# State-space mixer: a group's inputs and outputs turned between tokens and steps by 16 small ScalarE instructions instead of 16 TensorE products

## The reference

```python
def s5_mixer(h, w_in, ...):
    u = h @ w_in                                    # [256 tokens, 1024] = 64 groups of 16 channels
    for each chunk of steps:
        bu = einsum('bcgn,gpn->bcgp', u_c, bb)      # complex, 64 states a group
        s  = scan(s_t = lambda * s_{t-1} + bu_t)
        y  = real(einsum('bcgp,gnp->bcgn', s, c))
    y = y + d_skip * u
    g = gelu(y)
    g = g * sigmoid(g @ w_glu)
    return g @ w_out
```

## Time and profile before

| | |
|---|---|
| median of 3 runs | 1701.78 us (1699.98 to 1702.68) |
| the profiled execution | 1702.0 us, its span 1700.4 us |
| TensorE busy | 1682.7 us, 99% |
| VectorE busy | 1322.7 us, 78% |
| ScalarE busy | 875.4 us, 51% |
| GpSimd busy | 377.0 us, 22% |
| granted TensorE clock | full in all 40 slices |

### The profile page before, as it was taken

How to read it: one execution, slowest core, us unless ns; L and a number is a source line. 1 busy time by engine, 2 the same in 40 slices (tenths; PEclk the granted TensorE clock), 3 DMA queues, 4 the chain that set the end, 5 groups by cost and what they waited for, 6 DMA issues and landing times.

```text
span 1700.4 us, 29659 instructions
## 1 busy us (share of the span) xinstructions
PE 1682.7 (99%) x11608; PEld 1520.6 (89%) x11608; DVE 1322.7 (78%) x1813; ACT 875.4 (51%) x1280; POOL 377.0 (22%) x425
## 2 busy tenths in 40 slices
PE   9999999999999999999999999999999999999999
PEld 8899999898889998888888998888888899988887
DVE  7897889885868889787896868886688765678773
ACT  5875444353665444455544256554555435556552
POOL 0232012535514313600032130002100137330000
PEclk9999999999999999999999999999999999999999
DMA  8246567675116787555636445565455644335560
GB/s 336 94 146 216 202 212 271 231 270 197 60 50 217 250 270 268 183 201 179 227 142 260 130 154 184 182 242 176 145 201 199 221 151 169 122 127 199 200 244 25
DMA packets 50709, 320.98 MB, mean 189 GB/s; under 512 B 7696, under 2 KB 8912, under 8 KB 20144
## 3 DMA queue, kind: packets, MB, share of 16 engines
q1 hardware_dynamic: 36432, 280.61, 46.3%
q0 software_dynamic: 12736, 36.87, 6.8%
q10 hardware_dynamic: 1440, 2.10, 0.3%
HBM read 307.39 MB, written 10.09 MB: 187 GB/s over the span
## 4 chain that ended last, share of the span: by engine, by line
PE 89%; DVE 7%; DMA 2%; ACT 1%; issue 1%; POOL 0%; SPq 0%; ACTq 0%; DVEq 0%
PE bank L2363 35%; PE bank L2364 17%; PE bank L2357 9%; PE bank L2358 8%; PE bank L2359 8%; DVE w_lo L1495 2%; PE bank L2583 1%; PE bank L2690 1%; PE bank L3062 1%; PE bank L3014 1%; PE bank L2767 1%; PE bank L2596 1%; PE bank L2703 1%; PE bank L2880 1%; ACT w_hi L1041 1%
## 5 line engine op out<-in xcount | busy, mean ns | idle before, releaser
L1495 DVE TENSOR_TENSOR w_lo<-raw,w_hi 128x1024 fp32r<-128x1024 f32 (+2 forms) x486 | 640.8, 1321 | 178.5 <-ACT w_hi L1041 176.5
L1041 ACT ACTIVATE w_hi<-raw 128x1024 fp32r<-128x1024 f32 (+2 forms) x486 | 538.2, 1113 | 401.4 <-PE bank L2364 229.2
L2363 PE MATMUL bank<-hg,w_hi 128*128 128x512 f32 x1408 | 491.9, 395 | 0.0
L2364 PE MATMUL bank<-hg,w_lo 128*128 128x256 f32 x1408 | 391.6, 278 | 0.0
L2363 PE MATMUL bank<-hid,w_hi 128*128 128x512 f32 x1056 | 372.1, 396 | 2.5 <-DVE h L1540 1.5
L2357 PE MATMUL bank<-hg,w_hi 128*128 128x256 f32 x1240 | 354.2, 286 | 1.1 <-ACT u_s L1420 0.8
L2358 PE MATMUL bank<-hg,w_hi 128*128 128x256 f32 x1240 | 350.8, 283 | 0.0
L2359 PE MATMUL bank<-hg,w_lo 128*128 128x256 f32 x1240 | 350.7, 283 | 0.0
L2363 PEld LDWEIGHTS bank<-hg,w_hi 128*128 128x128 f32 x1408 | 264.2, 188 | 62.5
L2364 PE MATMUL bank<-hid,w_lo 128*128 128x256 f32 x1056 | 296.7, 281 | 0.0
L2364 PEld LDWEIGHTS bank<-hg,w_lo 128*128 128x128 f32 x1408 | 264.8, 188 | 0.1
(11 more groups left out here) (431 smaller groups left out, 2240.0 us busy)
## 6 DMA issues: line engine op xcount, KB each, us to landing
raw<-in_w SPq DMA_DIRECT2D x189, 1024.0 KB, 4.8
raw<-in_w SPq DMA_DIRECT2D x48, 1408.0 KB, 6.1
raw<-in_w SPq DMA_DIRECT2D x8, 768.0 KB, 4.8
b_rows<-in_s_b_rows POOLq DMA_DIRECT2D x8, 512.0 KB, 8.1
l_rows<-s_powers POOLq DMA_DIRECT2D x64, 64.0 KB, 9.2
s_ca<-cp_s POOLq DMA_DIRECT2D x8, 512.0 KB, 4.4
s_ba<-ba_s POOLq DMA_DIRECT2D x8, 512.0 KB, 7.4
ba_slot<-s_ba POOLq DMA_DIRECT2D x8, 512.0 KB, 5.5
```

The source lines that it names most:

```text
L1041: act.activation(w_hi[s][:, 0:n], raw[r][:, c * n:(c + 1) * n], ACT.Copy).then_inc(hi_made, 1)
L1495: dve.tensor_tensor(w_lo[s][:, 0:n], raw[r][:, c * n:(c + 1) * n], w_hi[s][:, 0:n].bitcast(F32), ALU.subtract).then_inc(lo_made, 1)
L2363: pe.matmul(psum[:, :].rearrange("p (a t) -> p a t", a=2), w_hi_ap, x_pair, start=first, stop=False)
L2364: return pe.matmul(psum[:, 0:T], w_lo_ap, x_pair[:, 0, :], start=False, stop=last)
```

## The change

All four `turn_inputs` and the first three `turn_outputs` leave TensorE. In their place ScalarE gets `turn_inputs(r)`: 16 activations, each of 32 partitions and 2 x 64 elements, which copy one step of one quarter of both tiles from `u_s` (every fourth element) to the 32 partitions of that step in `u4_s`. And it gets `gelu_to_steps(r)` for r = 0 to 2: 16 activations, each of which takes 32 partitions and 128 elements of the bank of `chunk_outputs(r)` through the gelu and writes them to every fourth element of `u_s`; then the high part is made as before. Group 3 keeps the old way out. TensorE's and ScalarE's orders are written anew, and on VectorE `keep_u(2)` goes ahead of `states(0)`.

```diff
--- before.py
+++ after.py
@@ -614,7 +614,6 @@
         z_read = sem("z_read")
         z_scanned = sem("z_scanned")
         h_made = sem("h_made")
-        u4_turned = sem("u4_turned")
         g_made = sem("g_made")
         g_turned = sem("g_turned")
         g_kept = sem("g_kept")
@@ -1400,10 +1399,32 @@
                     for j in range(a, b):
                         split_hi(half0 + j + SPLIT)
 
-                def keep_chunk_rows(r):
-                    act.wait_ge(u4_turned, r + 1)
-                    act.activation(u4_s[:, 2 * r:2 * r + 2, :, :], y_bank(r)[:, :].rearrange("p (k q c) -> p k q c", k=2, q=4), ACT.Copy)\
-                       .then_inc(u4_made, 1)
+                def quarter(i):
+
+                    return slice(32 * i, 32 * i + 32)
+
+                def turn_inputs(r):
+
+                    act.wait_ge(u_made, r + 1)
+                    for q in range(4):
+                        u = by_chunk(u_s[quarter(q), 2 * r:2 * r + 2, :])
+                        for step in range(LC):
+                            last = act.activation(u4_s[quarter(LC - 1 - step), 2 * r:2 * r + 2, q, :], u[:, :, :, step], ACT.Copy)
+                    last.then_inc(u4_made, 1)
+
+                def gelu_to_steps(r):
+
+                    if r == 0:
+                        act.wait_ge(half_used, half0 + 8)
+                    act.wait_ge(ca_used, 2 * r + 2)
+                    for q in range(4):
+                        g = by_chunk(u_s[quarter(q), 2 * r:2 * r + 2, :])
+                        for step in range(LC):
+                            y = y_bank(r)[quarter(step), :].rearrange("p (k q c) -> p k q c", k=2, q=4)
+                            last = act.activation(g[:, :, :, step], y[:, :, q, :], ACT.Gelu_apprx_tanh)
+                    last.then_inc(g_kept, 1)
+                    act.wait_ge(g_kept, r + 1)
+                    act.activation(hg_hi[:, 2 * r:2 * r + 2, :], u_s[:, 2 * r:2 * r + 2, :], ACT.Copy).then_inc(ghi_made, 1)
 
                 def gelu(r):
 
@@ -1413,9 +1434,7 @@
                                    ACT.Gelu_apprx_tanh).then_inc(g_made, 1)
 
                 def hi_of_g(r):
-                    if r == 0:
-                        act.wait_ge(half_used, half0 + 8)
-                    act.wait_ge(g_turned, r + 1)
+                    act.wait_ge(g_turned, 1)
                     g = u_s[:, 2 * r:2 * r + 2, :]
                     act.activation(g, two(y_bank(r)[:, :]), ACT.Copy).then_inc(g_kept, 1)
                     act.wait_ge(g_kept, r + 1)
@@ -1427,21 +1446,17 @@
                 split(0, 2)
                 root(ph["norm"])
                 split(2, 3)
-                keep_chunk_rows(0)
+                turn_inputs(0)
                 split(3, 5)
-                keep_chunk_rows(1)
+                turn_inputs(1)
                 split(5, 7)
-                keep_chunk_rows(2)
+                turn_inputs(2)
                 split(7, 8)
-                gelu(0)
-                keep_chunk_rows(3)
-                hi_of_g(0)
-                gelu(1)
-                hi_of_g(1)
-                gelu(2)
-                split(8, 9)
-                hi_of_g(2)
-                split(9, 11)
+                turn_inputs(3)
+                gelu_to_steps(0)
+                gelu_to_steps(1)
+                gelu_to_steps(2)
+                split(8, 11)
                 gelu(3)
                 hi_of_g(3)
                 split(11, 12)
@@ -2304,8 +2319,8 @@
                 split(2, 3)
                 keep_u(1)
                 split(3, 4)
+                keep_u(2)
                 states(0)
-                keep_u(2)
                 states(1)
                 keep_u(3)
                 states(2)
@@ -3019,24 +3034,10 @@
 
                     return s5_ident[:, 32 * q:32 * q + 32]
 
-                def turn_inputs(r):
-
-
-                    pe.wait_ge(u_made, r + 1)
-                    if r >= 2:
-                        pe.wait_ge(u4_made, r - 1)
-                    out = y_bank(r)[:, :].rearrange("p (k q c) -> p k q c", k=2, q=4)
-                    for q in range(4):
-                        for step in range(LC):
-                            row = LC - 1 - step
-                            last = pe.matmul(out[32 * row:32 * row + 32, :, q, :], rows_of(q),
-                                             by_chunk(u_s[:, 2 * r:2 * r + 2, :])[:, :, :, step], start=True, stop=True)
-                    last.then_inc(u4_turned, 1)
-
                 def turn_outputs(r):
 
 
-                    pe.wait_ge(g_made, r + 1)
+                    pe.wait_ge(g_made, 1)
                     out = y_bank(r)[:, :].rearrange("p (k c s) -> p k c s", k=2, s=LC)
                     for step in range(LC):
                         for q in range(4):
@@ -3051,8 +3052,6 @@
                     pe.wait_ge(h_made, 2 * r + 2)
                     if r >= 2:
                         pe.wait_ge(g_kept, r - 1)
-                    else:
-                        pe.wait_ge(u4_made, r + 3)
                     for kt in (2 * r, 2 * r + 1):
                         pe.wait_ge(ca_in[kt % 4], 16 * (kt // 4 + 1))
                         for q in range(4):
@@ -3094,25 +3093,18 @@
                 mean_square(ph["norm"])
                 u_half(1, 0)
                 u_half(1, 1)
-                turn_inputs(0)
                 u_half(2, 0)
+                u_half(2, 1)
                 chunk_inputs(0)
-                turn_inputs(1)
-                u_half(2, 1)
+                u_half(3, 0)
                 chunk_inputs(1)
-                u_half(3, 0)
-                turn_inputs(2)
                 u_half(3, 1)
                 chunk_outputs(0)
                 chunk_inputs(2)
-                turn_inputs(3)
-                turn_outputs(0)
                 chunk_outputs(1)
                 chunk_inputs(3)
-                turn_outputs(1)
                 chunk_outputs(2)
                 gate_products(0, (0, 1))
-                turn_outputs(2)
                 gate_products(1, (0, 1))
                 gate_products(2, (0, 1))
                 chunk_outputs(3)
```

## The result

The changed kernel takes 1707.3 us in the median of 12 runs (1704.87 to 1714.08), the kernel before beside it 1702.2 (12 runs): a ratio of 1.0036, 95% interval 1.0023 to 1.0049. The forecast was 1698.4, with a range of 1696.3 to 1703.6. The profiled execution took 1706.2 us, its span 1704.3; the page has

A forecast was written before the change was run, and what follows sets the result against it. TensorE was taken as the bound; removing 10.7 us from it, VectorE lets through at most 5.0, and ScalarE's chain leaves 17.0 - 5.0 - 8.6 = 3.4: 1701.8 - 3.4 = 1698.4 us, range 1696.3 to 1703.6.

The forecast's parts named there:

- I take no overlap: 0.31 and 0.27: ScalarE's small activations: assumed 0.31 us (inputs) and 0.27 us (gelus) from one start to the next, without overlap.
- the rival: ScalarE's small activations: every-fourth-element access is slower, kernel slower by 1.5 us, or 2.5 at double price; chance 0.16.
- The formula: ScalarE's chain to chunk_outputs(3): gain = 17.0 - 16 x input step - 32 x output step, never over 5.0 us.
- slower by 2.5: Small activations: if each strided element costs double, 0.105 us a step, the kernel takes 1704.3 us.
- VectorE lets through 5.0: VectorE's operations through the fourth states let chunk_outputs(3) start at 970.2 instead of 975.24: at most 5.0 us gained.
- ScalarE's chain 17.0: ScalarE's chain reaches chunk_outputs(3) at 958.2 plus the small steps, against 975.24: 17.0 us before subtracting those steps.
- TensorE's clock falls in the new waits: TensorE, rival: two groups at 1.2 GHz, about 9 us becoming 18, giving 1707 us; chance 0.04.
- The waits: TensorE would wait for VectorE about 0.9, 1.2, 1.9 and 1.9 us ahead of the four chunk_outputs.
- turn_inputs(0) must end by 918.8: ScalarE's first input turn: starts at 913.1, takes 5.0 us, ready at 918.1 with 0.7 us to spare.
- wanted at 925.5: ScalarE's turn_inputs(1): stands behind two weight halves, ends near 925.0, in time for 925.5.
- The table load: ScalarE's chain ahead of the gelus: 1.3 us, without the skill's 1.38 us drain; with it the gain would be 2.0.
- The coefficient loads: Tile 3's load lands at 926.6, wanted at 927.3; a microsecond late would fall into the 0.9 us wait: cost nothing.

The follow-up runs named there:

- e3: The changed kernel with each small activation reading and writing the same quarter, still every fourth element (values arranged otherwise): 1707.3 us, one run.
- e10: The changed kernel with fillers (products on constants into a free bank) at all of TensorE's waits in the stage: 1705.6 us, ratio 1.0028.
- e13: The changed kernel with small activations contiguous and on one quarter (values arranged otherwise), plus fillers ahead of the four chunk_outputs: 1697.4 us, ratio 0.9969.
- e14: The changed kernel with small activations on 64 elements in a row, quarters still changing (values land elsewhere), plus fillers in the expected waits: 1698.6 us, ratio 0.9979.
- e4: The changed kernel with small activations both contiguous and on the same quarter (values arranged otherwise), no fillers: 1707.1 us, ratio 1.0032.
- e2: The changed kernel with small activations on 64 elements in a row instead of every fourth, quarters still changing (values land elsewhere): 1707.8 us, ratio 1.0034.
- e11: The kernel before with only the inputs of groups 2 and 3 turned on ScalarE: 1699.0 us, ratio 0.9981.
- e12: The kernel before with inputs of groups 1 and 2 and outputs of group 2 turned on ScalarE, chunk_inputs(1) moved behind u_half(3, 0): 1699.6 us, ratio 0.9985.
- e18: e12 with three products on constants filling the wait ahead of chunk_inputs(2): 1697.1 us, ratio 0.9967.
- e17: e15 with three products on constants ahead of chunk_inputs(2) and three ahead of chunk_inputs(3): 1697.2 us, ratio 0.9972.
- e15: e12 with the inputs of group 3 turned on ScalarE too, waits left open: 1713.6 us, ratio 1.0073.
- e5: The kernel before with only the inputs turned on ScalarE, all outputs still on TensorE: 1703.6 us (1698.4 to 1710.8), ratio 1.0011.
- e16: e15 with two products on constants in the wait ahead of chunk_inputs(2) only: 1704.4 us, ratio 1.0009.
- e6: The kernel before with only the outputs of groups 0 to 2 turned on ScalarE, all inputs still on TensorE: 1707.9 us, ratio 1.0042.
- e1: The changed kernel with fillers at three waits, ahead of chunk_inputs(1), chunk_inputs(3) and chunk_outputs(2): 1707.2 us, ratio 1.0034.

## Why the prediction was wrong

- **"I take no overlap: 0.31 and 0.27"** is the step that failed first, as the text said it would. The part on overlap was right (a change of quarter costs 0.09, e3 against the change), the price of one instruction wrong: 433 and 395 ns against 308 and 268 when contiguous. The row on `blk_k` had shown such a cost on VectorE, 0.71 ns an element; on ScalarE it is 125 ns for 128, 0.98. I set TensorE's turn against it, which reads at the same step and looked fast enough, and gave the rival 0.16; ScalarE behaved like VectorE here and not like TensorE. By it the stage went from 3.4 us of gain to 3.8 of loss at the full clock (e10): 7.2 of the 10.0 us by which the stage missed the forecast.
- **The formula** stood. With 0.446 and 0.406 it gives 17.0 - 7.1 - 13.0 = -3.1, and the late first turn about 1 more; e10 showed 3.8 lost at the full clock. It was written for this case, "slower by 2.5" at double the price, and its terms (VectorE lets through 5.0, ScalarE's chain 17.0) were within 0.8 us (e13, e14).
- **"TensorE's clock falls in the new waits"**, put at nothing in the forecast and at a chance of 0.04, is the second step that failed. In the change it is the other 2.8 of the 10.0 us; with short steps it is the greater one, in e4 10 us, more than everything that the change could bring. Its price, 9 us for two groups, was near what e2 and e4 lost by it (9.2 and 9.7). The evidence against it was a wait of 1.6 us elsewhere in the kernel: one wait that passed is no measure, since here waits of equal length passed in one place or execution and not in another. Nor did I ask what the turns did for the clock while they were there. With the forecast's own steps, e2, the kernel would have come out at 1707.8 and not at 1698.4. Only with the clock held as well does the forecast come out (e14, 1698.6). That the median of the change, 1707.3, is the clock rival's 1707 is luck: there both steps failed, each by less.
- **The waits** for VectorE ahead of `chunk_outputs(0)` and `(1)` came out as laid out where ScalarE was not in the way: 1.04 and 1.09 us in e4, for 0.9 and 1.2. In the change itself 1.15, 2.42 and 3.62 us stand instead, all for ScalarE.
- **"turn_inputs(0) must end by 918.8"**: it took 7.1 us and TensorE waited 1.15 us for it. `turn_inputs(1)`, "wanted at 925.5", came later still, by 2.42 us, since it stands behind the first and two weight halves. These two were costed at nothing.
- **The table load** was 1.28 us (950.47), and the gelu began at 951.76. The drain that the Trainium skill has (ScalarE: Activation LUTs, What ACT_TABLE_LOAD costs) is not seen here.
- **The coefficient loads** had no wait in the changed kernel, as said. With the forecast's own steps, e2, one of 1.00 us stands ahead of tile 3; the prediction let such a microsecond fall into a later wait at no cost, and instead the clock was at 0.50 behind it.

The Trainium skill's rule on a changed quadrant (VectorE: DVE Perf Modes, two Vector instructions with no wait between them), written for VectorE, describes ScalarE here too: 0.446 us from start to start with a change of quarter, when one instruction takes 0.433 and so has ended, and 0.353 without it. Its note on cachelines (SBUF — State Buffer, Door 1) has the sign of the other cost; it gives no size, and the 0.125 us for 128 elements is from e2.

Open is why e10 scatters by 8 us at a mean clock of 0.999 and more: only one of its runs was profiled. Open too is what makes one wait bring the clock down and another of the same length not. Whether the fillers' width matters or their presence was not tried.

## What to carry to other kernels

Short products taken off TensorE leave waits behind, and a wait can cost its clock: before moving them, lay out the waits that remain, read the granted clock around each in the new trace, and move less or fill the wait where it falls. A wait that passed in one execution or one place is no proof for another. Move the pieces that nobody waits for at once; here two and three of the seven gained 3.1 and 2.7 us (e11, e12), three and four with the waits filled some 4.5 (e18, e17), four with the waits open lost 11 (e15), and all seven lost 5. Price a strided small instruction on the engine that will run it. Where a kernel's times fall into two groups, as in e5, look at the clock beside each run before calling the spread noise.

## What was not expected of the hardware

- TensorE's granted clock fell behind waits of 0.49, 0.64, 1.00 and 1.09 us with products of 64 columns right behind them (e16, e15, e2, e4), and didn't behind 1.04 us in e4, 0.98 us in e6, 0.81 us in the gate products of every version, or 1.6 us elsewhere. Behind 1.13 and 1.15 us ahead of `chunk_inputs(0)` it fell in e1 and e5, and behind 1.15 us at the same place in the change it didn't.
- It stayed low over 38 us in which TensorE never waited, while the chunk products and a 1 us turn ran, and came back within 3 us of the start of two turns in a row (e12) or during gate products (e15).
- ScalarE's copy of 32 x 128 elements takes 308 ns in a row and 433 with every fourth; a change of quarter adds 0.09 us from start to start.
